# Second-layer expert weights issued by ScalarE, first-layer weights by SyncE alone, and the last expert's second layer in two column halves

## The reference

```python
logits = (xf @ router_w).astype(jnp.float32) + router_b
top_v, top_i = lax.top_k(logits, TOP_K)          # 4 of 32 experts
gate = jax.nn.softmax(top_v, axis=-1)
...
hdn = xb @ w1[e] + b1[e]                         # 1024 -> 2048
g_, u_ = hdn[:, :D_FF], hdn[:, D_FF:]
g_ = jnp.minimum(g_, SWIGLU_LIMIT)
u_ = jnp.clip(u_, -SWIGLU_LIMIT, SWIGLU_LIMIT)
return ((u_ + 1.0) * (g_ * jax.nn.sigmoid(g_ * SWIGLU_ALPHA))) @ w2[e] + b2[e]   # 1024 -> 1024
```

## Time and profile before

| what | value |
|---|---|
| median of 3 runs | 1200.3 us (1198.89 to 1200.47) |
| the profiled execution | 1199.65 us |
| its span | 1197.8 us |
| granted TensorE clock | 0.998 of 2.4 GHz |
| TensorE busy | 1146.9 us, 96% |
| ScalarE busy | 218.0 us, 18% |
| VectorE busy | 287.4 us, 24% |
| moved by DMA | 429.67 MB, 427.15 of it by SP's queue |

### The profile page before, as it was taken

The page is one execution under the profiler, slowest core; times in us unless marked ns, Lnnn a source line. Parts: engine busy times, 40 slices in busy tenths (PEclk is TensorE's granted clock), DMA queues, the critical chain, the costliest instruction groups (busy, mean ns, idle before and its releaser), DMA issues.

```text
span 1197.8 us, 14564 instructions
## 1 busy us (share of the span) xinstructions
PE 1146.9 (96%) x5844; PEld 502.2 (42%) x5844; DVE 287.4 (24%) x742; ACT 218.0 (18%) x456; POOL 31.9 (3%) x67
## 2 busy tenths in 40 slices
PE   7999999999999999999999999999999999999997
PEld 6874878753333333333333333333333333333332
DVE  1368666662111111111111111111111111111113
ACT  1345554411111111111111111111111111111112
POOL 1000122100000000000000000000000000000000
PEclk9999999999999999999999999999999999999999
DMA  8525202288999999999999999999999999999994
GB/s 337 200 98 199 112 1 77 106 328 332 414 428 429 428 428 427 429 429 428 429 428 429 428 384 428 429 429 428 429 428 427 428 429 429 428 429 428 427 423 200
DMA packets 34474, 429.67 MB, mean 359 GB/s; under 512 B 3868, under 2 KB 4028, under 8 KB 8464
## 3 DMA queue, kind: packets, MB, share of 16 engines
q1 hardware_dynamic: 33296, 427.15, 85.0%
q0 software_dynamic: 432, 1.02, 0.3%
q10 hardware_dynamic: 720, 1.15, 0.3%
HBM read 428.25 MB, written 1.05 MB: 358 GB/s over the span
## 4 chain that ended last, share of the span: by engine, by line
PE 62%; DMA 30%; DVE 5%; ACT 1%; issue 1%; SPq 1%; POOLq 0%; POOL 0%; DVEq 0%
PE bank L1407 20%; DMA pool<-in_exp_w 17%; PE bank L1443 14%; DMA ring<-in_exp_w 13%; PE bank L990 5%; PE bank L1000 3%; PE bank L1379 3%; PE bank L1389 2%; PE bank L1289 2%; PE bank L1427 1%; DVE pool L2023 1%; DVE pool L2018 1%; DVE pool L2020 1%; PE bank L1160 1%; PE bank L1175 1%
## 5 line engine op out<-in xcount | busy, mean ns | idle before, releaser
L1443 PE MATMUL bank<-ring,pool 128*64 128x512 f32 x1024 | 228.1, 596 | 9.0 <-DMA ring<-in_exp_w 8.9
L1407 PE MATMUL bank<-ring,pool 128*64 128x512 f32 x1024 | 228.0, 595 | 5.7 <-DMA ring<-in_exp_w 5.5
L1407 PE MATMUL bank<-pool 128*64 128x512 f32 x1024 | 228.0, 595 | 5.8 <-DMA pool<-in_exp_w 5.6
L1443 PEld LDWEIGHTS bank<-ring,pool 128*64 128x64 f32 x1024 | 70.1, 137 | 165.2 <-issue 145.0
L1407 PEld LDWEIGHTS bank<-pool 128*64 128x64 f32 x1024 | 71.3, 137 | 157.8 <-issue 144.1
L1407 PEld LDWEIGHTS bank<-ring,pool 128*64 128x64 f32 x1024 | 71.2, 137 | 158.0 <-issue 143.1
L2004 DVE TENSOR_SCALAR pool<-pool 128x128 f32<-128x128 f32 x64 | 19.4, 345 | 428.0 <-PE bank L1407 428.0
L925 ACT ACTIVATE pool<-pool 128x512 f32<-128x512 f32 x32 | 20.2, 632 | 471.5 <-DVE pool L2016 471.5
L2016 DVE TENSOR_SCALAR pool<-bank 128x512 f32<-128x512 f32 x32 | 22.2, 693 | 316.1 <-PE bank L1407 316.1
L990 PE MATMUL bank<-pool,ring 128*128 128x256 f32 x272 | 62.0, 390 | 6.9 <-DMA ring<-in_w_in_C 6.9
L935 ACT ACTIVATE pool<-bank 128x512 f32<-128x512 f32 x32 | 19.2, 599 | 257.4 <-PE bank L1443 257.4
(11 more groups left out here) (304 smaller groups left out, 857.5 us busy)
## 6 DMA issues: line engine op xcount, KB each, us to landing
ring<-in_exp_w SPq DMA_DIRECT2D x126, 2048.0 KB, 22.2
pool<-in_exp_w SPq DMA_DIRECT2D x63, 2048.0 KB, 26.9
ring<-in_w_out SPq DMA_DIRECT2D x2, 2048.0 KB, 7.7
ring<-in_exp_w SPq DMA_DIRECT2D x4, 1024.0 KB, 14.3
ring<-in_w_in_A SPq DMA_DIRECT2D x1, 2048.0 KB, 13.3
ring<-in_w_in_B SPq DMA_DIRECT2D x1, 2048.0 KB, 7.7
ring<-in_w_in_D SPq DMA_DIRECT2D x1, 2048.0 KB, 13.3
ring<-in_w_in_H SPq DMA_DIRECT2D x1, 2048.0 KB, 8.1
```

The lines of the kernel that those rows point to most:

```text
L1407: last = mm(bank[4 + g][hp, :], lhs, w[:, k % 2, o:o + 512], start=False, stop=(k == KD - 1), skip_group_check=(k < 2))
L1443: last = mm(bank[6][SLOTS * hf:SLOTS * hf + SLOTS, :], hT[:, k % 4, SLOTS * (k // 4):SLOTS * (k // 4) + SLOTS], w2s[k // 4][:, k % 4, 512 ...
```

## The change

- ScalarE issues both second-layer pieces of expert e+1 from its own queue, right behind its copy of expert e's output. Its loop runs over 30 experts now, and the last two are written out. For the last expert it issues the second piece in two parts, as SP did.
- SP issues the first layer alone. `final_parts` and `AHEAD` are gone, and so are all calls of `last_parts` in the first pass. The second layer of expert 0 is still SP's.
- The last expert's second layer is computed in two column parts: first columns 0 to 255 of each half into bank 6, then columns 256 to 511 of each half into bank 7. ScalarE copies each part when it is done. The last `combine` is done in two parts as well.
- The first-layer bias products for the next expert, which the last expert did behind its second layer, are done at the start of a pass.
- VectorE multiplies by the sigmoid before it clips the up half.

The diff, cut to its core:

```diff
-AHEAD = 14
@@ SP
-            def final_parts(e, it):
-                sp.wait_ge(s_w2, it * 2 - 1)
-                load_slot(e, 4, False)
-                sp.wait_ge(s_w2, it * 2)
-                sp.dma_start(w2s[1][:, 0:2], ew2[e][1][:, 0:2]).then_inc(s_slot[5], 16)
-                sp.dma_start(w2s[1][:, 2:4], ew2[e][1][:, 2:4]).then_inc(s_end, 16)
             def from_second(it0, start):
-                with sp.Fori(start, AHEAD // 2) as e2:
+                with sp.Fori(start, NE // 2 - 2) as e2:
                     for odd in range(2):
                         e = e2 * 2 + odd
                         first_parts(e + 2, it0 + e + 2, odd)
-                        last_parts(e + 1, it0 + e + 1)
-                last_parts(AHEAD + 1, it0 + (AHEAD + 1))
-                with sp.Fori(AHEAD // 2, NE // 2 - 2) as e2:
-                    for odd in range(2):
-                        e = e2 * 2 + odd
-                        first_parts(e + 2, it0 + e + 2, odd)
-                        last_parts(e + 2, it0 + e + 2)
                 first_parts(NE - 2, it0 + (NE - 2), 0)
-                last_parts(NE - 2, it0 + (NE - 2))
                 final_first_parts(NE - 1, it0 + (NE - 1))
-                final_parts(NE - 1, it0 + (NE - 1))
...
-            last_parts(1, 1)
             first_parts(3, 3, True)
-            last_parts(2, 2)
@@ ScalarE
-                with act.Fori(0, NE) as e:
+                with act.Fori(0, NE - 2) as e:
+                    it = p * NE + e
+                    hidden_and_tokens(it)
+                    out_rows(it)
+                    for h in range(2):
+                        act.dma_start(w2s[h], ew2[e + 1][h]).then_inc(s_slot[4 + h], 16)
+                hidden_and_tokens(p * NE + (NE - 2))
+                out_rows(p * NE + (NE - 2))
+                act.dma_start(w2s[0], ew2[NE - 1][0]).then_inc(s_slot[4], 16)
+                act.dma_start(w2s[1][:, 0:2], ew2[NE - 1][1][:, 0:2]).then_inc(s_slot[5], 16)
+                act.dma_start(w2s[1][:, 2:4], ew2[NE - 1][1][:, 2:4]).then_inc(s_end, 16)
+                hidden_and_tokens(p * NE + (NE - 1))
+                act.wait_ge(s_wh, p + 1)
+                A(ysb[:, 0:256], bank[6][:, 0:256], ACT.Copy).then_inc(s_yh, 1)
+                act.wait_ge(s_w2, p * (2 * NE) + 2 * NE)
+                A(ysb[:, 256:512], bank[7][:, 0:256], ACT.Copy).then_inc(s_yev, 1)
@@ TensorE, the last expert
+                    out_bias(bank[6], 0, 256)
+                    pe.wait_ge(s_htev, it + 1)
+                    for k in range(KD):
+                        w2_ready(k)
+                        for hf in range(2):
+                            last = w2_rows(k, hf, bank[6], 0, 256, k == KD - 1)
+                    last.then_inc(s_wh, 1)
+                    pe.wait_ge(s_xs, it + 2)
+                    out_bias(bank[7], 256, 256)
+                    for k in range(KD):
+                        for hf in range(2):
+                            last = w2_rows(k, hf, bank[7], 256, 256, k == KD - 1)
...
-                if final is not None:
-                    bias_rows((0, 1), stop=True).then_inc(s_esu, 1)
...
+            pe.wait_ge(s_yh, npass)
+            for c in range(NCH):
+                combine(c, False, cols=slice(0, 256))
             pe.wait_ge(s_yev, npass * NE + 1)
             for c in range(NCH):
-                combine(c, True, s_all)
+                combine(c, True, s_all, slice(256, 512))
@@ VectorE
                     V.tensor_scalar(hr, bank[4][:, :], 7.0, None, ALU.min).then_inc(s_hg, 1)
+                    dve.wait_ge(s_hs, it + 1)
+                    V.tensor_tensor(hr, hr, sg, ALU.mult).then_inc(s_hm, 1)
                     dve.wait_ge(s_w1, it * 4 + 4)
                     V.tensor_scalar(ur, bank[5][:, :], 7.0, -7.0, ALU.min, ALU.max).then_inc(s_hu, 1)
-                    dve.wait_ge(s_hs, it + 1)
-                    V.tensor_tensor(hr, hr, sg, ALU.mult).then_inc(s_hm, 1)
```

More of the change, by code:

```diff
@@ L477, in encoder_kernel @@
         s_yev = sem("expert_out_evacuated")
+        s_wh = sem("last_expert_out_half_done")
+        s_yh = sem("last_expert_out_half_evacuated")
         s_xsr = sem("token_rows_evacuated")
@@ L921, in _, with hidden_and_tokens @@
             with act.Fori(0, npass) as p:
-                with act.Fori(0, NE) as e:
-                    it = p * NE + e
+                def hidden_and_tokens(it):
                     act.wait_ge(s_hg, it + 1)
@@ L1374, in gather_turn, with combine @@
                 last.then_inc(s_gtr2, 1)
-            def combine(c, stop, done=None):
+            def combine(c, stop, done=None, cols=slice(0, 512)):
                 for hf in range(2):
                     hp = slice(SLOTS * hf, SLOTS * hf + SLOTS)
-                    last = mm(bank[2 * c + hf][:, :], gT[hp, P * c:P * c + P], ysb[hp, :], start=False, stop=stop,
+                    last = mm(bank[2 * c + hf][:, cols], gT[hp, P * c:P * c + P], ysb[hp, cols], start=False, stop=stop,
                               skip_group_check=True)
@@ L1391, in bias_rows, with out_bias @@
                 return last
+            def out_bias(out, o, n):
+                gp = slice(2 * NE, 3 * NE)
+                for hf in range(2):
+                    mm(out[SLOTS * hf:SLOTS * hf + SLOTS, 0:n], esel[gp], bias[gp, 512 * hf + o:512 * hf + o + n],
+                       start=True, stop=False)
             def expert(it, turn, odd, final):
@@ L1431, in expert, with w2_ready @@
                 pe.wait_ge(s_gtev, it + 1)
-                bias_rows((2,))
-                pe.wait_ge(s_htev, it + 1)
-                if final is None:
-                    bias_rows((0, 1)).then_inc(s_esu, 1)
                 pe.wait_ge(s_again, 16)
-                for k in range(KD):
+                def w2_ready(k):
                     if k % 4 == 0:
@@ L1441, in expert, with w2_rows @@
                         pe.wait_ge(s_end, final)
-                    for hf in range(2):
-                        last = mm(bank[6][SLOTS * hf:SLOTS * hf + SLOTS, :],
-                                  hT[:, k % 4, SLOTS * (k // 4):SLOTS * (k // 4) + SLOTS],
-                                  w2s[k // 4][:, k % 4, 512 * hf:512 * hf + 512], start=False, stop=(k == KD - 1))
-                    if k % 4 == 3:
-                        last.then_inc(s_w2, 1)
-                if final is not None:
-                    bias_rows((0, 1), stop=True).then_inc(s_esu, 1)
+                def w2_rows(k, hf, out, o, n, stop):
+                    return mm(out[SLOTS * hf:SLOTS * hf + SLOTS, 0:n], hT[:, k % 4, SLOTS * (k // 4):SLOTS * (k // 4) + SLOTS],
+                              w2s[k // 4][:, k % 4, 512 * hf + o:512 * hf + o + n], start=False, stop=stop)
+                if final is None:
+                    out_bias(bank[6], 0, 512)
+                    pe.wait_ge(s_htev, it + 1)
+                    bias_rows((0, 1)).then_inc(s_esu, 1)
+                    for k in range(KD):
+                        w2_ready(k)
+                        for hf in range(2):
+                            last = w2_rows(k, hf, bank[6], 0, 512, k == KD - 1)
+                        if k % 4 == 3:
+                            last.then_inc(s_w2, 1)
+                else:
+                    out_bias(bank[6], 0, 256)
+                    pe.wait_ge(s_htev, it + 1)
+                    for k in range(KD):
+                        w2_ready(k)
+                        for hf in range(2):
+                            last = w2_rows(k, hf, bank[6], 0, 256, k == KD - 1)
+                    last.then_inc(s_wh, 1)
+                    pe.wait_ge(s_xs, it + 2)
+                    out_bias(bank[7], 256, 256)
+                    for k in range(KD):
+                        for hf in range(2):
+                            last = w2_rows(k, hf, bank[7], 256, 256, k == KD - 1)
+                        if k % 4 == 3:
+                            last.then_inc(s_w2, 1)
             pe.wait_ge(s_sel, 1)
```

1 line of the change is left out of this document (added).

## The result

The changed kernel takes **1208.97 us** (median of 4 runs, 1208.65 to 1209.08). The kernel before, in 4 runs on the same chip, takes 1199.86 us. The ratio is 1.0071, with a 95% interval of 1.0058 to 1.0084. The forecast was 1204.5 in a range of 1197 to 1211: the sign is right, but the loss is twice the 4.2 us of the sum. The profiled execution took 1209.08 us with a span of 1207.3, so 9.5 us of span have to be found.

The account below looks back on a forecast made before the run. DMA transfers at 428 GB/s were taken to bound the kernel from 526 us, TensorE before. Terms -3.0 + 3.0 + 5.3 - 0.9 - 0.2 = +4.2 us gave 1203.9, stated as 1204.5 us for the median, range 1197 to 1211.

Parts of the forecast that it names:

- The limit and the rate: From 526 us on, transfers at 428 GB/s set the pace; the change leaves volume and rate alone.
- the rival of a higher rate: From 306 to 1180 us, two queues move more bytes, 8.7 us faster per percent; chance 0.17.
- The hole at 697 us: Where SP's first loop ends, the DMA engines no longer run dry: -3.0 us.
- The hole at 304 us: Expert 1's second layer is issued later, behind ScalarE's copy, so the engines idle longer: +3.0 us, range 1.7 to 4.1.
- The order at the end: Expert 30's second layer takes bandwidth from its last first-layer piece, delaying the end: +5.3 us, bounds 0 and 9.8.
- the rows of both kinds are 16 KB, so each queue gets half: Near the end, queues alternate by packet with equal rows, so 1.1 second-layer pieces pass ahead; equal turns had chance 0.55.
- the last w2 lands early, its slack wasted: At the end, the last expert's second-layer weights arrive before they are wanted, which gains nothing; no separate size.
- The halves of the last layer: After the last second layer, column halves let copy and combination overlap: -0.9 us.
- The swap: VectorE multiplies before clipping, saving TensorE waits of 0.11 us an expert, counted only in the last two: -0.2 us.
- Never for w2: TensorE stops for first-layer piece 3 from about 680 us on, but never for second-layer weights; a sign without size.
- Service in order of issue: At the end, pieces move in the order both engines issued them, so no delay: 1199.2 us, chance 0.08.
- Second layer first: At the end, up to two whole second-layer pieces jump ahead, 9.8 us instead of 5.3: 1209 us, chance 0.12.

Follow-up runs that it names:

- e2: Changed kernel with the second-layer loads of experts 28 to 31 back on SP's queue in the earlier order: 1199.92 us, ratio 0.9994.
- e1: Changed kernel with only expert 31's second layer back on SP's queue, behind the last first-layer piece: 1203.66 us, ratio 1.0022.
- e4: Changed kernel with the last first-layer piece of expert 31 issued whole, in 16 KB rows: 1204.54 us, ratio 1.0029.
- e6: Changed kernel with all weight loads on SP's queue as before, keeping column halves and VectorE's swap: 1201.49 us, ratio 1.0002.
- e5: Kernel before with only VectorE's swap, multiplying by the sigmoid before clipping: 1200.93 us, ratio 0.9996.
- e7: Changed kernel with each second-layer piece issued as two loads with 8 KB rows instead of 16: 1280.95 us, one run.
- e8: Changed kernel with second layers of experts 1 and 28 to 31 on SP's queue, and the last layer's column halves interleaved: 1196.79 us, ratio 0.9967.
- e10: Changed kernel with all weight loads as before and the last second layer's column halves interleaved: 1199.60 us, ratio 0.9990.

## Why the forecast had the sign and half the size

**The limit and the rate: right.** 428 GB/s from 300 us to the end with one queue or two; the rival of a higher rate is out. The queues moved 297 and 131 MB, as forecast.

**The hole at 697 us, -3.0: right.** Both windows read 426 GB/s.

**The hole at 304 us, +3.0: right in transfers, 2.7.** The step behind it had one fault: the issue was put at 306.2, behind the copy. The trace of ScalarE has it at 305.58, while the copy that began at 305.43 still runs:

```profile
305.43 0.60 ACT L921 ACTIVATE pool<-bank 128x512 f32<-128x512 f32 x1 [7.62 <-PE bank L1452]
305.58 0.88 ACTq L929 DMA_DIRECT2D ring<-in_exp_w  x2
```

That is the low bound of the forecast (the issue does not wait for the copy), and alone it would have made 1.7 to 2.7 of the 2.3 to 3.3 us. What was measured is the upper end of that: the restart was as ragged as the forecast feared, 197 and 131 GB/s from 306 to 308 us. The landings, 10.2 and 19.5 us after the issue where 7.6 was assumed for a lone piece, tell nothing of the hole, since SP issues pieces again from 308.85 us on and takes its share. What a microsecond of this hole costs at the end stays open, as said above.

**The order at the end, +5.3: right, 4.6 measured.** The stop before 30(3) ends 1146.75 - 1142.13 = 4.6 us later. The working holds piece by piece: from 1146.75 to about 1180.8 us at 4.9 a piece, 6.9 pieces were outstanding, the number that the forecast derived from equal turns, and between 1132.8 and 1146.7 us ScalarE's queue moved 2.15 MB, 1.0 piece where the forecast had 1.1. Undoing it in e2 gave T30 back to 1156.7 from e1's 1162.5.

**The step that failed: "the rows of both kinds are 16 KB, so each queue gets half".** It is true of 30(3) and of all the steady run, and false for 31(3), which the code issues in 4 KB rows. The rule of equal turns had been read from a stretch where one queue had 16 KB rows and the other 2 KB, so it was known that row sizes set the shares; I applied it at one place and then took "the last w2 lands early, its slack wasted" as the end of the matter, without asking whom that early arrival displaces. The rule at the second place would have said: w2(31), issued from 1161.99 us on, is served alongside 31(3), and takes a row of 16 or 8 KB for each row of 4 KB. The missing term is +5.9 us: 4.0 of stops and 2.1 of low clock, less 0.2. e4 and e1 measured it by the ratios at 5.0 and 5.9; in their traces T30 to T31 is 28.9 and 27.3 us where the changed kernel has 33.7.

**The low clock** was not in the forecast at all. Behind the stops of 2.18 and 1.80 us the level was 0.50 for about 4 us. In e1 and e4, without the pair of stops, it stays at 1.00 in the same place. So the 4.0 us of waits cost 6.1. That it takes a pair is not shown: before 1130 us the changed kernel has eight single stops of 2.2 to 2.6 us, and behind four of them (794.96, 853.70, 941.80 and 1000.52 us) the next 16 products take 5.35 us at the low level, behind the other four some 3.65. Two of the eight in the chain, one of each kind:

```profile
853.70 5.35 PE bank L1418 x16
...
1059.26 3.65 PE bank L1418 x16
```

**The halves of the last layer, -0.9: right.** T31 to the end is 0.9 shorter. But VectorE's statistics are now on the chain, where ScalarE's work was: they start 1.54 us behind T31 (1197.16) where they started 2.11 behind it. Columns cost nearly the same in halves, twice 3.60 us for 7.02. The forecast left out that the last quarter is wanted 3.5 us earlier, which costs 1.3 us as soon as w2(31) is last in line (e2, e6).

**The swap, -0.2: no more than that can be told** (e5: 0.9996, interval 0.9987 to 1.0006). TensorE gains 0.37 us an expert and not 0.11.

**"Never for w2": wrong, at no cost.** TensorE first stops for piece 3 of the first layer at 677 us, as forecast, but it also stops six times for the second half of the second layer, four of them between 411 and 495 us, 0.3 us at most and 1.6 in all. The chain of the changed kernel shows it there:

```profile
387.94 23.32 DMA ring<-in_exp_w
...
411.30 3.68 PE bank L1452 x16
```

With 0.6 us for the issue, that is a loop of 27.7 us (439.01 - 411.30 in the next round) where the forecast had 26.5, and TensorE's own work is 27.16. The loop of the second layer was thus closer to being the bound than I thought. It is hidden, since from 498 us on the transfers need 29.4 us an expert.

**The other rivals.** Service in order of issue is refuted by the equal counts of e7. "Second layer first", at 1209, hit the number, but not by its mechanism: it had two whole pieces ahead of 30(3), and the trace has 1.0; that the measured 1208.97 meets its number is chance.

## What to carry to other kernels

When loads move to a second queue, do not look only at volume and rate. Ask for the last few pieces which ones are in flight together, and which the compute wants first: within one queue the order is yours, between the two queues here it was turns, one row each, so a load in small rows lost to one in large rows in the ratio of their sizes. A second queue cost nothing measurable in the steady part, where the transfers were the limit and the rows equal; for the last experts, where nothing later can hide a late piece, put all of it back on one queue in the order of use (e2, e8). And where a product is split in columns, keep the operand that arrives last out of the first part for as long as possible (e8, e10).

## What the runs showed of the hardware

- Two queues shared the DMA engines by equal counts of packets, one row of the load each, over 140 us within 1% (2584 and 2563), with 2.02 times the bytes on the side with rows twice as long. In steps of 0.2 us the turns of the changed kernel show singly at 560 us: groups of 15 to 17 packets, 0.6 us each, over 16 engines.
- ScalarE began the issue behind its own copy 0.15 us after the copy began, not after it ended (305.58 and 305.43), and at 1161.99 us 0.01 us after it (1161.98).
- TensorE's granted clock fell to 0.50 behind two stops of about 2 us each that lay 2 us apart, and was back at 1.00 from 1186 us. In the steady part it fell behind four of eight single stops of 2.2 to 2.6 us in the changed kernel and behind none of 1.5 us or less; the kernel before stops for up to 1.2 us there and stays at 1.00. Stretches of 40 us with such a fall (760 to 800, 840 to 880, 920 to 960, 1000 to 1040) have a mean of 0.96. What it costs is hidden there while the transfers set the pace (428 GB/s throughout).
- The transfer rate was the same with one queue and with two: 428 to 429 GB/s from 340 to 660 us in the kernel before, the changed kernel and every run but e7, whose engines ran short of work (401 to 405).
